# Eight ring buffers for the U gathers and six for the V gathers, in place of seven and seven

## What is computed

```
q = (xb @ w_q)                                  # 8 heads, two halves each
t1, i1 = top_k(q1 @ keys_1, 16); t2, i2 = top_k(q2 @ keys_2, 16)
top, sel = top_k(t1 + t2, 16)                   # 16 experts a head
g = softmax(top)
u = take(expert_u, idx); a = gelu(einsum('thkd,td->thk', u, xb))
y = einsum('thk,thkd->td', g * a, take(expert_v, idx))
```

## Time and profile before

| | |
|---|---|
| median of 3 executions | 3385.03 us |
| the profiled execution, its own time | 3354.33 us |
| its span (first to last instruction) | 3352.6 us |
| TensorE matmuls busy | 2349.4 us (70%) |
| VectorE busy | 2147.1 us (64%) |
| ScalarE busy | 535.9 us (16%) |
| GpSimd busy | 1992.9 us (59%) |
| mean granted TensorE clock | 0.74 |
| moved by the software DMA queue (the gathers) | 1107.43 MB |

### The profile page before, as it was taken

One profiled execution on the slowest core, in us unless ns is written; L12 is line 12 of the kernel. 1 busy time (PEld: TensorE's weight loads), 2 busy tenths in 40 slices (PEclk: granted clock), 3 DMA queues, 4 the chain that ended last, 5 costly groups with the idle time before them and its releaser, 6 DMA issues.

```text
span 3352.6 us, 42363 instructions
## 1 busy us (share of the span) xinstructions
PE 2349.4 (70%) x15147; PEld 1174.5 (35%) x15147; DVE 2147.1 (64%) x5579; ACT 535.9 (16%) x1059; POOL 1992.9 (59%) x2128
## 2 busy tenths in 40 slices
PE   8995775667667888877857765668567765675545
PEld 4652352335233533334534432325223431221111
DVE  1257757776676656657577667676676676766653
ACT  2211111211121221112121111111111111210001
POOL 0036666666666566665666666666666666666665
PEclk9996796678566988987867776678676875566555
DMA  6479999999999999999999999999999999999998
GB/s 229 149 277 405 358 349 375 362 373 349 375 357 381 368 402 408 408 400 357 362 353 365 366 369 363 360 372 351 376 361 374 364 353 377 359 359 362 368 368 325
DMA packets 348955, 1197.59 MB, mean 357 GB/s; under 512 B 37760, under 2 KB 54408, under 8 KB 346952
## 3 DMA queue, kind: packets, MB, share of 16 engines
q0 software_dynamic: 304128, 1107.43, 87.8%
q1 hardware_dynamic: 44616, 87.45, 7.1%
HBM read 1180.69 MB, written 14.15 MB: 356 GB/s over the span
## 4 chain that ended last, share of the span: by engine, by line
PE 31%; issue 16%; POOL 14%; DVE 13%; DMA 10%; another core or an unknown queue 9%; DVEq 5%; ACT 1%; ACTq 0%; SPq 0%; POOLq 0%
PE mx L1574 9%; PE acc L1675 7%; POOL ring L597 7%; POOL ring L586 7%; DVE ring L1273 6%; DMA ring<-in_peer_v_dram,idx 4%; PE mx L1385 3%; DMA ring<-in_peer_u_dram,idx 3%; DVEq L1145 2%; PE acc L1361 2%; PE mx L1585 2%; PE mx L1556 1%; DMA weights<-in_w_in_dram 1%; PE h2p L1628 1%
## 5 line engine op out<-in xcount | busy, mean ns | idle before, releaser
L1273 DVE SCALAR_TENSOR_TENSOR ring<-ring,h2p 128x1024 f32<-128x1024 f32 x1056 | 1272.2, 1214 | 551.7 <-DMA ring<-in_peer_u_dram,idx 267.5
L1675 PE MATMUL acc<-ring,wk 128*32 128x256 f32 x8448 | 1030.7, 507 | 684.6 <-DMA ring<-in_peer_v_dram,idx 317.5
L597 POOL DMA_INDIRECT ring<-in_peer_v_dram,idx x1056 | 995.3, 942 | 790.6 <-remote 369.4
L586 POOL DMA_INDIRECT ring<-in_peer_u_dram,idx x1056 | 995.8, 943 | 554.7 <-issue 302.4
L1675 PEld LDWEIGHTS acc<-ring,wk 128*32 128x32 f32 x8448 | 316.5, 129 | 1316.5 <-issue 776.9
L1574 PE MATMUL mx<-reg,weights 128*128 128x128 f32 x1792 | 275.3, 309 | 42.4 <-issue 42.1
L1574 PEld LDWEIGHTS mx<-reg,weights 128*128 128x128 f32 x1792 | 245.8, 216 | 101.5 <-issue 101.1
L1556 PE MATMUL mx<-weights,reg 128*128 128x512 f32 (+1 forms) x256 | 138.6, 668 | 1.9 <-DVEq L1246 1.1
L1385 PE MATMUL mx<-weights 128*128 128x512 f32 (+1 forms) x288 | 132.4, 604 | 2.2 <-issue 1.4
L1628 PE MATMUL h2p<-ch,ident 32*32 32x512 f32 x528 | 104.4, 798 | 31.2 <-issue 20.2
L828 ACT ACTIVATE gl<-dots 128x16 f32<-128x16 f32 x66 | 14.2, 216 | 537.8 <-issue 368.5
(11 more groups left out here) (311 smaller groups left out, 2425.6 us busy)
## 6 DMA issues: line engine op xcount, KB each, us to landing
ring<-in_peer_u_dram,idx POOLq DMA_INDIRECT x1056
ring<-in_peer_v_dram,idx POOLq DMA_INDIRECT x1056
weights<-in_peer_w_q_dram SPq DMA_DIRECT2D x7, 2048.0 KB
weights<-in_w_in_dram SPq DMA_DIRECT2D x5, 2048.0 KB, 18.2
weights<-in_w_in_dram SPq DMA_DIRECT2D x10, 1024.0 KB
ring<-in_peer_w_q_dram SPq DMA_DIRECT2D x8, 1024.0 KB, 6.1
xt<-in_x_prompt_dram SPq DMA_DIRECT2D x8, 512.0 KB
ring<-in_w_out_dram SPq DMA_DIRECT2D x2, 2048.0 KB, 13.6
```

The costliest lines, as they stand in the source:

```text
L586: pool.indirect_dma_start(ring[:, U_AT[n % NU], :], None, u_d, bass.IndirectOffsetOnAxis(ap=idx[:, g % 4, k:k + 1], axis=0)).then_inc(u_in ...
L597: pool.indirect_dma_start(ring[:, V_AT[n % NV], :], None, v_d, bass.IndirectOffsetOnAxis(ap=idx[:, g % 4, k:k + 1], axis=0)).then_inc(v_in ...
L1273: V.scalar_tensor_tensor(ring[:, U_AT[n % NU], :], ring[:, U_AT[n % NU], :], 1.0, h2p[:, :], ALU.mult, ALU.mult, accum_out=dots[:, (g + 1) ...
L1675: last = T.matmul(sums[g // 2 % 2][j * SUB:(j + 1) * SUB, :], wk[:, n // FEW % 5, n % FEW, :], ring[:, V_AT[n % NV], j * QD:(j + 1) * QD], ...
```

## The change

The ring keeps its 14 buffers. U gets eight of them and V six: `U_AT` gains place 12, `V_AT` loses it. With that the general waits become: U gather n waits for dot product n - 8, and V gather n for the matmuls of V buffer n - 6. The order of the gathers stays.

Of the staging buffers, number 5 is now the first half of U buffer 7 (place 12, where number 8 was), 6 and 7 are the halves of V buffer 4 (place 10), 8 and 9 those of V buffer 5 (place 11); the units' table follows. U gathers 6 and 7 wait for the stores out of 4 and 5, V gather 4 for those out of 6 and 7, V gather 5 for those out of 8 and 9.

```diff
-NU = 7
-NV = 7
-U_AT = [0, 1, 2, 3, 4, 5, 13]
-V_AT = [6, 7, 8, 9, 10, 11, 12]
+NU = 8
+NV = 6
+U_AT = [0, 1, 2, 3, 4, 5, 13, 12]
+V_AT = [6, 7, 8, 9, 10, 11]
...
-UNIT_PO = [(0, 1, 2, 3, 4, 8)[n % 6] for n in range(BEHIND)] + [4, 5, 6, 7, 8, 9, 5, 6, 10, 11, 12]
+UNIT_PO = [(0, 1, 2, 3, 4, 5)[n % 6] for n in range(BEHIND)] + [4, 6, 7, 8, 9, 6, 7, 8, 10, 11, 12]
...
-        po += [ring[:, U_AT[6], 0:512]] + [ring[:, V_AT[4], 0:512]] + [a[:, h * 512:h * 512 + 512] for a in (ring[:, V_AT[5], :], ring[:, V_AT[6], :]) for h in range(2)]
+        po += [ring[:, U_AT[6], 0:512], ring[:, U_AT[7], 0:512]] + [a[:, h * 512:h * 512 + 512] for a in (ring[:, V_AT[4], :], ring[:, V_AT[5], :]) for h in range(2)]
...
                     pool.wait_ge(u_free, n - NU + 1)
                 elif n == 4:
                     pool.wait_ge(query_ready, 3)
-                elif n == 6:
-                    pool.wait_ge(proj_out[4], stored(4, len(UNITS)))
+                elif n >= 6:
+                    pool.wait_ge(proj_out[n - 2], stored(n - 2, len(UNITS)))
...
                     pool.wait_ge(v_free, n - NV + 1)
-                elif n >= NV - 3:
-                    for b in {NV - 3: (5,), NV - 2: (6, 7), NV - 1: (8, 9)}[n]:
+                elif n >= NV - 2:
+                    for b in {NV - 2: (6, 7), NV - 1: (8, 9)}[n]:
                         pool.wait_ge(proj_out[b], stored(b, len(UNITS)))
```

## The result

The kernel with eight U slots and six V slots takes 3394.72 us (median of 12 runs, 3383.68 to 3404.1), the kernel before, on the same chip, 3386.77 (12 runs, 3380.8 to 3392.92). The ratio is 1.0021, 95% interval [1.0011, 1.0031]: slower by 7 us by the ratio and by 8 between the medians, where 137 were forecast (3524 less 3386.77). A difference of the two traces is 40 us, and only a fifth of that is in the medians. The traces tell where buffers are waited for; the ratios tell what it costs.

What follows compares the result with a forecast made beforehand. Neither GpSimd nor DMA rate fills the time; GpSimd loses about 0.4 us a pair waiting for buffers, mostly V. 144 + 6 - 12 = +138 us on 3354.33, times 1.0092, gives 3524 us (+4.1%), range 3400 to 3700.

Steps and rivals of the forecast that it cites:

- V is the ring that is waited for: GpSimd's net waits before gathers: 452 us for V buffers against 38 us for U, so V is short by twelve to one.
- Step 1: V gather n waits for product n - 6, not n - 7: one pair, 2.48 us, in 58 groups, +144 us.
- GpSimd cannot win it back: At each longer stop GpSimd loses a pair, 2.48 us, for good: 1.24 us a gather against the DMA engines' 1.29.
- The cover: How long a TensorE stop can last before GpSimd is held: 11.3 us with seven V buffers, 14.9 - 6.1 = 8.8 with six.
- lower bound: Step 1 costs 0 us if VectorE and TensorE are far enough behind the arrivals; L1273 waited only 185 times in 1056.
- the quarter: Part of step 1 left if VectorE's backlog hides most of it: 36 us, +30 us in all, 3415 us.
- The stretch from 1200 to 1500 us costs nothing: Six groups left out of step 1: DMA engines are full there, so a late issue only shortens the queue.
- Step 2: After the last U gather, about 12 V gathers at 2.08 us each in place of 1.56: +6 us (0 to +8).
- Step 3: U gather n waits for product n - 8; half of 23 us net U waits given back, -12 us (-23 to 0).
- Step 4: The late units' staging buffers: same copies and stores in other halves, SyncE's work and order unchanged, 0 us.
- The scale of 1.0092: Median shown, 3385.03 us, lies 0.92% above the profiled execution's 3354.33; it takes the forecast from 3492.3 to 3524 us.
- The rival "absorbed": Mechanism right, but VectorE's backlog hides most of step 1: +30 us, 3415 us; chance 22%.

Runs made afterwards that it cites:

- seven and six slots: Seven U and six V buffers, one slot unused, against the kernel before: 3391.85 us, 1.0027 on the chip of 3384 us; 3119.38 us, 1.0025 on that of 3113.
- the move the other way: Six U and eight V buffers against the kernel before: 3458.64 us, 1.0245 on the chip of 3384 us; 3114.71 us, 1.0009 on that of 3112.
- five slots: Nine U and five V buffers against the kernel before: 3404.0 us, 1.0056 on the chip of 3384 us; 3141.93 us, 1.0091 on that of 3113.
- bare stream: The 2112 gathers alone into 14 buffers, all consumers removed, against the kernel before: 2960.59 us, 0.875; on the chip of 3113 us 2729.41 us, 0.8765.
- Half gathers: Kernel before with each gather bringing 256 KB in place of 512 KB, on a chip of 3113 us: 2926.73 us, 0.9405 of the kernel before.
- half dots: Kernel before with dot products over 512 of each U row's 1024 numbers, on a chip of 3113 us: 3096.68 us, 0.9949 of the kernel before.
- short V products: Kernel before with V products over 32 of each 256 columns, on a chip of 3113 us: 3107.37 us, 0.9983 of the kernel before.

## Why the prediction was wrong

The sign and the places were right, the size wrong by a factor of nearly twenty (137 us forecast, 7 to 8 measured).

- *V is the ring that is waited for, and the cost lies there.* Right as a reading, and confirmed by seven and six slots: 1.0027 and 1.0025 with no U slot added. Wrong as a measure of worth: on the first chip the move the other way costs nine times as much.
- *Step 1, +144 us.* This is the step that failed: 58 stops, each at the price of a pair. The count came from one stop of 10.1 us, which was taken for that of every change of group. It is the stop at the spreading of rows, which TensorE makes in every second group only. In the trace of before the time from one V product to the next is over 8.8 us 42 times in all and between 8.8 and 11.3 us, where cover would be lost, 27 times; at the spreading the median is 6.0 us. So 27 x 2.48 = 67 us would have been the sum, near the +70 us of net V waits between the traces (that the two agree may be luck).
- *The price, "GpSimd cannot win it back".* It failed too: of 70 us more at V gathers only 7 to 8 us are in the medians. It rested on GpSimd's 1.24 us against the DMA engines' 1.29, that is, on gathers having to run near their top rate to catch up. But a late gather need not be won back where its row would have stood in line: the rows stood 2 us less before VectorE and TensorE took them up. The cover took the hold as fixed; it went from 16.5 to 14.4 us. And five slots, where the same price asks 161 us more, cost 10 to 12 (22 on the other chip). The prediction had this as its lower bound ("behind the arrivals far enough that a later one costs nothing") and read the row for it, but gave it 22%. The chance was mis-set, and so was the quarter: a quarter of step 1 would be 36 us, and the medians show a total of 8.
- *The stretch from 1200 to 1500 us costs nothing.* Wrong in the traces: 10 us are lost between 1200 and 1500 us and 3 more up to 1560, 9 of them in the last 80 us. A missing buffer leaves less in the DMA queue, and at the next long stop of TensorE it ran dry sooner, as the shares of 0.70 and 0.72 show.
- *Step 2, +6 us at the end.* Too large. From the 12th V gather from the end to the last it is 17.4 us after and 16.3 before, +1.2 us.
- *Step 3, -12 us of U waits.* In the waits it is there (38 to 14 us net), but seven and six slots show the same 34.4 us, so it is not the eighth slot's doing. That U gathers wait less because the V wait ahead of them has grown is the likely reason, not shown.
- *Step 4, 0 us.* Nothing in the traces or the ratios speaks against it.
- *The scale of 1.0092 from one execution to the median.* It would have been better to doubt the execution: it is below all timed runs of its kernel, and its 2.94 us a pair are a good case, not the usual one.
- *The rival "absorbed"* is nearest to what the runs bear out on the first chip, with rows standing before TensorE as well as before VectorE. Its test in the prediction (V waits longer, time within 1%) is met, except that L1273's idle time grew as well (551.7 to 627.2 us). On the other chip the same 7 us come with another line, that before the DMA engines.

**What stays open.** What sets the pace on the chip of 3384 us. The bare stream takes 2.8 us a pair there and the kernel 2.94, and the ratio of the bare stream to the kernel is the same on both kinds of chip (0.875 and 0.8765), which suggests that the gathers' stream sets both. But in the bare stream the time is GpSimd's own 1.08 us, and in the kernel it is 0.94 with waits for buffers instead; and the kernel before reaches 407 GB/s on that chip for a while the earlier trace rows, which the bare stream does no more after about its first tenth. A high busy share of the DMA engines is no sign of a full queue there: at a share of 0.99 the first packet of a gather in the bare stream starts about 3.5 us after the gather (packets in order, as above), on the other chip about 10.3 us. Half gathers, half dots and short V products never ran on the chip of 3384 us. Nor is it shown why U buffers are dear there (1.0245 against 1.0009). TensorE's granted clock may have a part in the numbers of the first chip: its mean is 0.746 before, 0.731 with seven and six slots and 0.716 with nine and five, but 0.733, 0.731 and 0.730 on the other. As the first V buffer costs 7 to 8 us on both, the clock isn't needed for that.

## What to carry to other kernels

Before you price a buffer by the waits for it, ask how long the data in it stands untouched after it lands: where rows stand in line, a buffer less shortens the line and not the throughput, and hold divided by the number of buffers is a result of the pace, not its cause. Count how often a stop occurs before you multiply one by the number of groups. Run the transfers alone, with no consumer, before arguing about rings: that tells what a better ring could give back, here some 5%, and where the next line stands; it sets no bound on what a worse ring costs. And hold the profiled execution against the timed runs; differences between two traces can be several times the difference of the medians.

## What the runs showed of the hardware that was not expected

- *Chips differ by 8%* on the same kernel (3384 and 3112 us), and on the bare gathers by as much (2961 and 2729 us).
- *Releases by TensorE.* On the first chip the sign that a V product is done often comes long after its recorded end (11 us in the earlier trace rows), and GpSimd's "remote" waits of 369 us are these. In the trace of before 296 V gathers stand idle for more than 0.4 us, and they start 5.2 us (median, up to 14.8) after the recorded end of the product that they need. VectorE's releases are not late there: the 29 U gathers that waited so, the first of each group left out, start 0.27 us after the end of their dot product. On the other chip no V wait of the change is put down to "remote", and the gather follows the product's end by its plain 0.30 us (median of 139). The Trainium skill's "TensorE: Matmul & The Clock Gate", section "Single matmul latency", has a single bf16 matmul of N columns over (219 + N) / 1.2 ns after its start at the lower clock, which for 256 columns is an estimate of 0.4 us; the products here are fp32. Releases within a fraction of a us, as on the second chip, are of that order, those on the first are not. The lateness goes with the chip, then, and not with the kernel; the cause is not shown.
- *GpSimd's time for a gather* grew from 0.94 us (until 200 us) to 1.10 (from 280 us on) in the bare stream of the first chip, 1.08 on average, and only there.
- *One late part of a transfer.* In the bare stream at 410 GB/s the first fifteen of a gather's 16 landing signs come within 0.9 us of each other and the last one 5.0 us later (medians). It is the last that GpSimd waits for.
- *The rate.* A single core draws 410 GB/s in 4 KB rows on one chip; on the other it does so for the first slices and then 375, where GpSimd's gathers take longer. The Trainium skill's "DMA: Bandwidth & Descriptors", section "Where 436 GB/s comes from", lets reads from HBM end near 358 GB/s for each core. Both measurements are above that, the first by 15%. In its section "Measured (HBM→SBUF, 128 partitions, SWDGE, issued from GpSimd)" the same page of the Trainium skill gives such a share for the case that the neighbouring core streams too; no run here shows what the neighbour did.
